# The branch products of the dilated and the memory heads as seven block products each

## The reference

```python
y_a = jnp.einsum('bse,ed->bsd', o_a * jax.nn.silu(dg), w_br_diff)   # differential heads, 1024 wide
y_b = jnp.einsum('bse,ed->bsd', o_b * jax.nn.silu(lg), w_br_dil)    # dilated heads, 512 wide
y_m = jnp.einsum('bse,ed->bsd', o_m * jax.nn.silu(mg), w_br_mem)    # memory heads, 512 wide
gates = jax.nn.sigmoid(mgate).reshape(B, S, N_BRANCH, D_MODEL)
merged = gates[:, :, 0] * y_a + gates[:, :, 1] * y_b + gates[:, :, 2] * y_m
return x + jnp.einsum('bsd,de->bse', merged, w_out)
```

## Time and profile before

| what | value |
|---|---|
| median of the runs | 2078.49 us (2075.92 to 2079.03, three runs) |
| the profiled execution | 2080.16 us, of which the span from first to last instruction is 2078.3 us |
| busy over the span | PE 1822.0 us (88%), DVE 756.2 us (36%), ACT 385.1 us (19%), POOL 127.6 us (6%) |
| mean granted clock of TensorE | 0.956 |

### The profile page before, as it was taken

How to read it: one execution, slowest core, us unless ns; L and a number is a source line. 1 busy time by engine, 2 the same in 40 slices (tenths; PEclk the granted TensorE clock), 3 DMA queues, 4 the chain that set the end, 5 groups by cost and what they waited for, 6 DMA issues and landing times.

```text
span 2078.3 us, 35046 instructions
## 1 busy us (share of the span) xinstructions
PE 1822.0 (88%) x15030; PEld 1208.6 (58%) x15030; DVE 756.2 (36%) x1288; ACT 385.1 (19%) x889; POOL 127.6 (6%) x186
## 2 busy tenths in 40 slices
PE   8998776777699877766769999999999999999998
PEld 4756455455557555554554588746554588746553
DVE  5651111111144111111105503473757503474656
ACT  4511011011022101100112112222221112222121
POOL 1200000000000000000001401200221001200000
PEclk9999988988899989889989999999999999999999
DMA  8599999999999999999998863443646563443331
GB/s 334 177 365 415 419 421 420 420 420 420 420 397 378 420 420 421 420 420 420 420 419 311 178 202 129 135 162 122 172 154 210 118 206 127 137 153 130 132 122 61
DMA packets 155639, 588.62 MB, mean 283 GB/s; under 512 B 16468, under 2 KB 34260, under 8 KB 106456
## 3 DMA queue, kind: packets, MB, share of 16 engines
q1 hardware_dynamic: 146936, 567.45, 70.9%
q0 software_dynamic: 8544, 18.89, 3.7%
HBM read 577.90 MB, written 8.39 MB: 282 GB/s over the span
## 4 chain that ended last, share of the span: by engine, by line
PE 62%; DMA 17%; SPq 12%; DVE 6%; issue 2%; ACT 1%; DVEq 0%; ACTq 0%
PE ps L640 17%; DMA ring<-in_moe_w_dram 16%; PE ps L607 15%; SPq L1397 8%; PE ps L1677 5%; SPq L1406 4%; PE ps L1657 3%; PE ps L1712 3%; PE ps L613 2%; PE ps L584 1%; PE ps L1968 1%; PE ps L617 1%; PE ps L523 1%; PE ps L557 1%; PE ps L1732 1%
## 5 line engine op out<-in xcount | busy, mean ns | idle before, releaser
L1677 PE MATMUL ps<-ring,xT 128*32 128x128 f32 x8192 | 302.8, 306 | 177.9 <-DMA ring<-in_moe_w_dram 171.9
L1677 PEld LDWEIGHTS ps<-ring,xT 128*32 128x32 f32 x8192 | 262.9, 121 | 243.7 <-DMA ring<-in_moe_w_dram 186.1
L607 PE MATMUL ps<-xT,ring 128*128 128x256 f32 x1408 | 310.1, 380 | 0.0
L607 PEld LDWEIGHTS ps<-xT,ring 128*128 128x128 f32 x1408 | 265.3, 190 | 39.7 <-issue 4.9
L2394 DVE TENSOR_TENSOR arena<-arena,ps 128x256 f32<-128x256 f32 x32 | 13.5, 421 | 558.3 <-ACT arena L2062 558.3
L1089 DVE TENSOR_TENSOR ring<-ring 128x2048 f32<-128x2048 f32 x64 | 146.7, 2292 | 15.6 <-PE ps L640 6.9
L640 PE MATMUL ps<-ring,xT 128*128 128x512 f32 x336 | 151.1, 594 | 0.5 <-ACT xT L774 0.5
L1712 PE MATMUL ps<-arena 128*32 128x512 f32 x768 | 120.1, 607 | 31.6 <-DVE arena L2394 31.6
L1330 POOL DMA_DIRECT2D ring<-gap_bias x160 | 96.4, 672 | 796.9 <-DMA ring<-in_w_in_dram 475.4
L1657 PE MATMUL ps<-arena,x_tm 128*128 128x128 f32 x1024 | 137.3, 291 | 0.0
L1657 PEld LDWEIGHTS ps<-arena,x_tm 128*128 128x128 f32 x1024 | 128.9, 205 | 10.8 <-issue 10.7
(11 more groups left out here) (316 smaller groups left out, 2003.0 us busy)
## 6 DMA issues: line engine op xcount, KB each, us to landing
ring<-in_moe_w_dram SPq DMA_DIRECT2D x287, 1024.0 KB, 26.1
arena<-in_moe_w_dram SPq DMA_DIRECT2D x89, 1024.0 KB, 26.8
ring<-in_w_in_dram SPq DMA_DIRECT2D x44, 2048.0 KB, 8.5
ring<-in_w_in_dram SPq DMA_DIRECT2D x16, 1024.0 KB, 12.1
ring<-in_w_br_diff_dram SPq DMA_DIRECT2D x4, 2048.0 KB, 10.5
ring<-in_w_out_dram SPq DMA_DIRECT2D x4, 2048.0 KB, 8.0
arena<-in_moe_w_dram SPq DMA_DIRECT2D x14, 512.0 KB, 15.6
ring<-in_w_mem_kv_dram SPq DMA_DIRECT2D x3, 2048.0 KB, 18.9
```

The costliest lines, as they stand in the source:

```text
L607: m = nc.tensor.matmul(bank[:, u * T:(u + 1) * T], w[:, k, f * P:(f + 1) * P], xT[:, k, :], start=(k == 0), stop=(k == KD - 1))
L1677: m = nc.tensor.matmul(ps[SL * q:SL * q + SL, g % 2, s * P:(s + 1) * P], xs[:, g % 2, k, s * SL:(s + 1) * SL], w[:, c0:c0 + 2 * P - 1:2], ...
```

## The change

The four products of four matmuls of each of the two chunks become seven block products ("units") of two matmuls each. The tokens' features give blocks a11, a12, a21, a22 (128 tokens by 256 features), the weight gives b11, b21, b12, b22 (256 features by 512 columns). The combinations are

- of the tokens: s1 = a21 + a22, s2 = s1 - a11, s3 = a11 - a21, s4 = a12 - s2;
- of the weight: first = b12 - b11, second = b22 - first, third = b22 - b12 (written over b12), fourth = b21 - second (over b21);

and the units are 0: a11 b11, 1: s4 b22, 2: a12 b21, 3: s1 first, 4: s2 second, 5: a22 fourth, 6: s3 third. PE runs them in the order 0, 3, 2, 4, 1, 6, 5. Units 0, 3, 2 and 1 take turns in banks 0 and 1; units 4 and 6 use bank 3 one after the other and unit 5 uses bank 4. ScalarE copies units 0 and 3 out. VectorE makes the combinations, adds the products up and gates the sums with the two instructions as before. What moves besides: VectorE's token combinations and `first` stand in the pair ahead, before its last `add_product` (`br_begin`); `second` stands between the head's maximum and its reciprocal; and `first_out_w` moves from the middle of the memory products to the start of `out_rest`.

The core of the diff:

```diff
@@ PE @@
+            def br_product(l, i, u):
+                (a11, a12, _, a22), (s1, s2, s3, s4), (b11, b21, b12, b22), (first, second) = br_parts(i)
+                if u == 0:
+                    wait_chunk(pe, l, i)
+                    pe.wait_ge(sem("turn_read"), turns(l, BRANCHES[i]) + TILES[BRANCHES[i]] // 2)
+                if u in (3, 4, 6, 5):
+                    pe.wait_ge(sem("combined"), combined_for(l, (i, {3: "first", 4: "second", 6: "sum", 5: "fourth"}[u])))
+                if u < 4:
+                    n = AT[i, BR_RING.index(u)]
+                    pe.wait_ge(taken_of(l, n), products(l, n) // 2 + 1)
+                x_, w = ((a11, b11), (s4, b22), (a12, b21), (s1, first), (s2, second), (a22, b21), (s3, b12))[u]
+                for k in range(KH // 2):
+                    m = nc.tensor.matmul(ps[:, br_bank(l, i, u), :], x_[:, k, :], w[:, k, :],
+                                         start=(k == 0), stop=(k == KH // 2 - 1))
+                m.then_inc(sem("bank_full"), 1)
...
-                for half in range(3):
-                    product(l, LASTS - 1, half)
+                for u in BR_UNITS[:6]:
+                    br_product(l, LASTS - 1, u)
                 turn_merged(l, 0)
-                product(l, LASTS - 1, 3)
+                br_product(l, LASTS - 1, 5)
@@ ACT @@
+            def br_copies(l, i):
+                first, _, third = br_sums
+                for half, dst in ((0, first), (1, third)):
+                    n = AT[i, half]
+                    act.wait_ge(sem("bank_full"), filled(l, n + 1))
+                    nc.scalar.copy(dst, ps[:, bank_at(l, n), :]).then_inc(taken_of(l, n), 1)
@@ DVE, in the pair ahead @@
+                    if i + 2 in BRANCHES:
+                        br_begin(i + 2)
                     add_product(i, 6, first_part)
@@ DVE @@
                 def out_rest():
+                    first_out_w()
...
+                def br_begin(i):
+                    v.wait_ge(sem("turn_read"), turns(l, BRANCHES[i]) + TILES[BRANCHES[i]] // 2)
+                    (a11, a12, a21, a22), (s1, s2, s3, s4), (b11, _, b12, _), (first, _) = br_parts(i)
+                    ch(nc.vector.tensor_tensor(s1, a21, a22, ALU.add))
+                    ch(nc.vector.tensor_tensor(s2, s1, a11, ALU.subtract))
+                    ch(nc.vector.tensor_tensor(s3, a11, a21, ALU.subtract))
+                    ch(nc.vector.tensor_tensor(s4, a12, s2, ALU.subtract))
+                    combined()
+                    wait_chunk(v, l, i)
+                    ch(nc.vector.tensor_tensor(first, b12, b11, ALU.subtract))
+                    combined()
+
+                def br_second(i):
+                    _, _, (_, _, _, b22), (first, second) = br_parts(i)
+                    ch(nc.vector.tensor_tensor(second, b22, first, ALU.subtract))
+                    combined()
+
+                def br_gate(t, c, part):
+                    cols = slice(c * CW, (c + 1) * CW)
+                    g, m = gates[:, t, cols], merged[:, t, cols]
+                    ch(nc.vector.scalar_tensor_tensor(g, g, 1.0, part, ALU.add, ALU.mult))
+                    ch(nc.vector.tensor_tensor(m, m, g, ALU.add))
+
+                def br_rest(i):
...
+                    ch(nc.vector.tensor_tensor(b12, b22, b12, ALU.subtract))
+                    combined()
+                    wait_tanh(4)
+                    v.wait_ge(sem("bank_full"), br_filled(l, i, 2))
+                    wait_product_taken(v, l, AT[i, 0])
+                    ch(nc.vector.tensor_tensor(sum_, first_sum, bank(2), ALU.add))
+                    br_gate(0, 0, sum_)
+                    v.sem_inc(taken_of(l, AT[i, 2]), 1)
+                    ch(nc.vector.tensor_tensor(b21, b21, second, ALU.subtract))
+                    combined()
+                    v.wait_ge(sem("bank_full"), br_filled(l, i, 4))
+                    ch(nc.vector.tensor_tensor(sum_, first_sum, bank(4), ALU.add))
+                    combined()
+                    wait_product_taken(v, l, AT[i, 1])
+                    ch(nc.vector.tensor_tensor(first_sum, sum_, third, ALU.add))
+                    v.wait_ge(sem("bank_full"), br_filled(l, i, 1))
+                    ch(nc.vector.tensor_tensor(first_sum, first_sum, bank(1), ALU.add))
+                    br_gate(0, 1, first_sum)
+                    if tile_done:
+                        v.sem_inc(sem("merged_ready2"), 1)
+                    v.wait_ge(sem("bank_full"), br_filled(l, i, 6))
+                    ch(nc.vector.tensor_tensor(sum_, sum_, bank(6), ALU.add))
+                    ch(nc.vector.tensor_tensor(third, third, sum_, ALU.add))
+                    br_gate(1, 1, third)
+                    v.wait_ge(sem("bank_full"), br_filled(l, i, 5))
+                    ch(nc.vector.tensor_tensor(sum_, sum_, bank(5), ALU.add))
+                    br_gate(1, 0, sum_)
+                    if tile_done:
+                        v.sem_inc(sem("merged_ready2"), 1)
+                    v.sem_inc(taken_of(l, AT[i, 3]), 1)
...
                     if job:
                         scale_max(*job, job_n)
+                    if i in BRANCHES:
+                        br_second(i)
+                    if job:
                         weigh(*job, job_n)
```

More of the change, by code:

```diff
@@ L114 @@
     COMBOS += (["diff x"] if _i == DIFF_PAIR else []) + [(_i, j) for j in range(4)]
+    if _i + 2 in BRANCHES:
+        COMBOS += [(_i + 2, what) for what in ("x", "first", "second", "third", "fourth", "sum")]
 OUT_COMBOS = ["first w", "second w", "s1", "s2", "s4", "fourth w", "third w", "s3"]
@@ L608, in product @@
                                                  start=(k == 0), stop=(k == KD - 1))
-                elif name in ("br_dil", "br_mem"):
-                    x_, w = (obT if name == "br_dil" else omT), cslots_wide[s]
-                    t, cc = half // 2, half % 2
-                    for k in range(KD // 2):
-                        m = nc.tensor.matmul(bank, x_[:, k, t * P:(t + 1) * P], w[:, k, cc * CW:(cc + 1) * CW],
-                                             start=(k == 0), stop=(k == KD // 2 - 1))
                 else:
@@ L723, in pe_second @@
                         scores(l, *job, job_n)
-                    if chunk[0] == "br_dil":
-                        pe.wait_ge(sem("turn_read"), turns(l, "dil") + TILES["dil"] // 2)
-                    ahead = 2 if chunk[0] == "br_dil" else 1
-                    for half in range(ahead):
-                        product(l, i, half)
+                    if i in BRANCHES:
+                        for u in BR_UNITS[:3]:
+                            br_product(l, i, u)
+                    else:
+                        product(l, i, 0)
                     if job:
@@ L732, in pe_second @@
                         turn_after(l, after)
-                    for half in range(ahead, HALVES[i]):
-                        product(l, i, half)
+                    if i in BRANCHES:
+                        for u in BR_UNITS[3:]:
+                            br_product(l, i, u)
+                    else:
+                        for half in range(1, HALVES[i]):
+                            product(l, i, half)
                     if job:
@@ L901, in act_second @@
                         continue
+                    if i in BRANCHES:
+                        br_copies(l, i)
                     if job:
                         exps(l, *job, job_n)
-                    take(l, i, 0)
+                    if i not in BRANCHES:
+                        take(l, i, 0)
                     if job:
@@ L909, in act_second @@
                         take_after(after)
-                    for half in range(1, HALVES[i]):
+                    for half in range(1, 1 if i in BRANCHES else HALVES[i]):
                         take(l, i, half)
@@ L1307, in dve_second @@
                         combine_x(chunk_of("br_diff", 0))
-                    for half in range(HALVES[i]):
-                        take(i, half)
-                        if chunk[0] == "br_mem" and half == 2:
-                            first_out_w()
+                    if i in BRANCHES:
+                        br_rest(i)
+                    else:
+                        for half in range(HALVES[i]):
+                            take(i, half)
                     if job:
```

57 lines of the change are left out of this document (38 added, 19 removed).

## The result

The changed kernel takes 2093.57 us (median of 4 runs, 2092.0 to 2096.16); the kernel before, timed beside it, 2077.26 (2075.92 to 2079.03). The ratio is 1.0074, its 95% interval 1.0062 to 1.0087: slower by some 15 us by the ratio (the medians themselves differ by 16.3), where 2090.7 had been forecast in a range of 2084 to 2097. The profiled execution took 2092.21 us (span 2090.2, mean granted clock 0.957).

A forecast was written before the change was run, and what follows sets the result against it. PE was taken to bound the heads, with PE and VectorE arriving together at each layer's end. Losses of 1.5 and 4.6 us per layer, 12.2 in all, raise 2078.49 to 2090.7 us; range 2084 to 2097.

The forecast's parts named there:

- Removed work: In the four heads, 14 of 16 matmuls stay each: 1.72 us less PE work per head, 6.9 us in all.
- The price of the 1024 combination: On VectorE in each head: a weight combination of 1024 elements takes 1.22 us, from a line through three sizes.
- Dilated head: First changed head per layer: unit 6 waits 2.6 us for VectorE's sum; PE ends 1.3 us late.
- F: Moment in each layer from which the memory head is counted, the preceding pair's end; PE to reach it 1.5 us late.
- Memory head and output stage: From F to the layer's end: VectorE's queue is 4.6 us late, and PE's last two products wait for it.
- s3: In the output stage, the VectorE step that PE's last two products wait for; PE to wait some 2 us there.
- The sum: Both layers: 1.5 us up to F plus 4.6 after it, 6.1 us per layer, 12.2 us in all.
- rival 1: PE's clock falls in some new waits, 1.6 us each: 2093.9 us with one per layer, 2097.1 with two; chance 0.20.
- The rule of the Trainium skill: On PE's new waits of 1.2 to 2.6 us: gaps between bursts of matmuls return the clock to half rate.
- rival 2: In heads and output stage VectorE keeps up and PE's saving of 6.9 us comes through: 2071.6 us; chance 0.07.
- (3): Only the layer's end is late: dilated head keeps its 1.7 us, end loses 4.6; 2084.3 us; chance 0.08.
- (4): Over the whole kernel, losses and saving cancel: within 0.2% (4.2 us) of the time before; chance 0.05.

The follow-up runs named there:

- experiment 9: Against the kernel before: only the dilated head in seven products, its weight combinations set where VectorE was idle or awaiting exponentials; 2075.57 us, ratio 0.9984.
- 4: Against the changed kernel: TensorE computes unit 1 of each head twice into the same bank; 2092.75 us, ratio 1.0071.
- 5: Against the changed kernel: VectorE computes the first combination of w_out twice in each layer; 2097.77 us.
- 6: Against the changed kernel: TensorE computes half of the output stage's product 2 twice, just ahead of its wait; 2094.08 us.
- experiment 7: Against the changed kernel: the four weight combinations of each head moved from VectorE to GpSimd; 2102.02 us, ratio 1.0114.

## Why the prediction was right, step by step

**Removed work.** 4 matmul records fewer per head at the same 0.43 us: right. It shows as time only in experiment 9.

**The price of the 1024 combination.** 1.22 taken, 1.23 measured; the line through three sizes held.

**Dilated head.** Unit 6 was to wait 2.6 us and TensorE to be 1.3 late: 2.3 and 1.24 measured (from unit 0 to the values 2007.97 - 1990.85, less the 1.70 of the clock fall, 15.42 us; before, 2000.86 - 1986.68 = 14.18). The second pair was charged 0.2 and cost nothing: F 1.25 late for 1.5.

**Memory head and output stage.** The waits were to be 0.5, 1.2, 1.3, and about 2 twice: they are 0.22, 1.12, 1.03, 2.06 and 1.08. The last, at s3, is half of what was said; the time did not hang on it, since the sum took the end from VectorE's lateness and not from the waits. The second combination of w_out was to end at F + 23.4: it ends at 2057.17 + 2.29, F + 23.49. The end was to be 4.6 late and is 4.7. That this is VectorE's queue and not TensorE is shown by 4, 5 and 6.

**The sum.** 6.1 a layer forecast, 5.97 measured where the clock did not fall. The time of 2093.57 us lies inside the range, but above the 2087.5 to 2093 of the forecast itself and next to the 2093.9 of rival 1 with a clock fall in each layer. The profiled execution has one fall in the second block, so part of that closeness is chance. What the trace shows beyond the forecast are two things. First, rival 1 is partly true: behind one of the two waits in the dilated heads the clock fell to the lower level, for 1.70 us where 1.6 had been reckoned for each fall. It comes on top of the forecast, and not in its place. The rule of the Trainium skill that was weighed there (TensorE: Matmul & The Clock Gate, "Why this matters for your kernels") holds in direction: the rows could not yet say what a wait of 2.6 us does. Second, 0.6 to 0.7 us in layer 1 ahead of the changed part, at two waits for VectorE (0.36 us at 1626.42 and 0.32 at 1852.54, the last two lines of the table of waits) in pairs that the change does not touch, where the prediction had said that nothing would be lost elsewhere. VectorE has a hole of 0.50 us ahead of both, behind an instruction of its own, with nothing named that it waited for. The kernel before has such a hole at 1972.63, where VectorE's next wait for TensorE takes it up. The cause of the holes is open; the kernels with one head changed don't show these two waits.

**The other rivals.** VectorE does not keep up (2), and the loss is not at the end alone (3): the dilated head by itself costs 1.0012 to 1.003. Nor do losses and saving cancel (4): the interval begins at 1.0062. But rival 2's point of decision, the sum of unit 4 by the end of unit 1, was the right one: where experiment 9 meets it, the gain comes. That rival's other half, w_out by F + 18.8, was not met by any kernel here that changes the memory head.

## What to carry to other kernels

Fewer matmuls for more VectorE work paid here only where VectorE had idle time ahead of its next deadline, so look for the hole in which each added instruction is to stand; the share of busy time over the stage (9.5 of 17 us) does not tell. An operation that needs only weights can go into such a hole early, a sum that needs a product cannot, which is why the dilated head could be saved and the memory head, with the output stage right behind it, was not by any order tried here. If a wait shrinks when instructions change places and the time does not, look for where the wait came back before changing their order once more.

## What the runs showed of the hardware

- GpSimd is no place for spare tensor work beside a busy VectorE: in experiment 7 VectorE's 0.69 us became 2.7 and its 2.29 became 4.0 with both operands in SBUF, while a sum with one operand in PSUM and a maximum over a single operand kept their 0.69.
- The clock after a short wait is not certain. In the second block of the changed kernel and the eleven others TensorE waited 28 times for 2.0 to 2.6 us, and the granted clock fell around the work that followed in 13 of these cases, to 0.50, for about 1.7 us of lost time (5.40 us in place of 3.70); the same wait in the same kernel did it in one layer and not in the other. In all 8 waits of 4.4 to 5.5 us it fell, in none of the 161 of 0.3 to 1.3.
